# Third layer's attention with scores as split products, two heads side by side in the rows of the array, and the division of the probabilities on GpSimd

## The reference, cut to what matters

```python
q = (rms_norm(c_q, q_norm_w) @ w_uq).reshape(b, l, 16, 64 + 32)
kv = (rms_norm(c_kv, kv_norm_w) @ w_ukv).reshape(b, l, 16, 64 + 64)
q = jnp.concatenate([q_nope, rope(q_pe)], axis=-1)
k = jnp.concatenate([k_nope, jnp.broadcast_to(rope(k_pe), (b, l, 16, 32))], axis=-1)
s = jnp.einsum('bqhd,bkhd->bhqk', q, k) * (96 ** -0.5)
p = jax.nn.softmax(s, axis=-1)
return jnp.einsum('bhqk,bkhd->bqhd', p, v)
```

## Time and profile before

| what | value |
|---|---|
| median of 3 runs | 1498.38 us (1496.53 to 1502.21) |
| profiled execution: its own time | 1499.47 us |
| its span | 1497.6 us |
| TensorE (PE) busy | 95% of the span |
| VectorE, ScalarE, GpSimd busy | 54%, 44%, 55% |
| mean granted TensorE clock | 0.971 |

### The profile page before, as it was taken

One profiled execution on the slowest core, in us unless ns is written; L12 is line 12 of the kernel. 1 busy time (PEld: TensorE's weight loads), 2 busy tenths in 40 slices (PEclk: granted clock), 3 DMA queues, 4 the chain that ended last, 5 costly groups with the idle time before them and its releaser, 6 DMA issues.

```text
span 1497.6 us, 22626 instructions
## 1 busy us (share of the span) xinstructions
PE 1418.1 (95%) x8800; PEld 1212.4 (81%) x8800; DVE 812.0 (54%) x1554; ACT 666.3 (44%) x1100; POOL 825.7 (55%) x665
## 2 busy tenths in 40 slices
PE   5989999999999999887999999999999999999997
PEld 3868788999988887544878888888878865999997
DVE  3687667777576687567675333321126657332211
ACT  3445655544543133674442322232226376544442
POOL 0533507999864443554435454544446630699995
PEclk9999999999999999888999999999999999999999
DMA  9656605777775652100445555543333320365664
GB/s 367 258 184 232 256 5 195 261 253 253 239 262 186 203 175 85 42 29 1 150 146 197 197 186 195 186 140 90 104 104 101 114 96 1 113 195 186 184 185 125
DMA packets 71322, 242.59 MB, mean 162 GB/s; under 512 B 7472, under 2 KB 13104, under 8 KB 70832
## 3 DMA queue, kind: packets, MB, share of 16 engines
q1 hardware_dynamic: 68800, 237.15, 47.0%
q10 hardware_dynamic: 2416, 4.00, 0.9%
HBM read 239.02 MB, written 1.05 MB: 160 GB/s over the span
## 4 chain that ended last, share of the span: by engine, by line
PE 51%; DVE 3%; ACT 1%; issue 1%; POOL 0%; DMA 0%; DVEq 0%; ACTq 0%
PE bank L547 15%; PE bank L549 14%; PE bank L548 14%; PE cond_a L968 1%; PE bank L968 1%; PE bank L684 1%; PE bank L685 1%; PE bank L976 1%; PE cond_a L1028 1%; PE bank L688 1%; PE bank L988 1%; PE cond_b L988 1%; PE cond_b L976 0%; ACT w_hi L1286 0%; DVE scratch L2585 0%
## 5 line engine op out<-in xcount | busy, mean ns | idle before, releaser
L1794 POOL TENSOR_TENSOR w_lo<-raw,w_hi 128x512 fp32r<-128x512 f32 (+1 forms) x612 | 773.1, 1291 | 630.6 <-ACT w_hi L1286 619.7
L1286 ACT ACTIVATE w_hi<-raw 128x1024 fp32r<-128x1024 f32 (+3 forms) x301 | 308.9, 1029 | 592.5 <-PE bank L549 511.9
L547 PE MATMUL bank<-h_hi,w_hi 128*128 128x256 f32 (+2 forms) x1604 | 524.7, 327 | 5.9 <-DVE h_lo L1856 2.6
L549 PE MATMUL bank<-h_hi,w_lo 128*128 128x256 f32 (+2 forms) x1604 | 521.4, 325 | 0.0
L548 PE MATMUL bank<-h_lo,w_hi 128*128 128x256 f32 (+2 forms) x1604 | 521.3, 325 | 0.0
L547 PEld LDWEIGHTS bank<-h_hi,w_hi 128*128 128x128 f32 (+1 forms) x1604 | 301.9, 188 | 38.0 <-DVE h_lo L1856 5.8
L549 PEld LDWEIGHTS bank<-h_hi,w_lo 128*128 128x128 f32 (+1 forms) x1604 | 301.9, 188 | 26.4
L548 PEld LDWEIGHTS bank<-h_lo,w_hi 128*128 128x128 f32 (+1 forms) x1604 | 302.1, 188 | 26.0
L547 PE MATMUL bank<-hidden_hi,w_hi 128*128 128x256 f32 (+1 forms) x528 | 167.0, 316 | 0.2 <-POOL w_lo L1794 0.2
L548 PE MATMUL bank<-hidden_lo,w_hi 128*128 128x256 f32 (+1 forms) x528 | 166.9, 316 | 0.0
L549 PE MATMUL bank<-hidden_hi,w_lo 128*128 128x256 f32 (+1 forms) x528 | 166.9, 316 | 0.0
(11 more groups left out here) (416 smaller groups left out, 1771.7 us busy)
## 6 DMA issues: line engine op xcount, KB each, us to landing
raw<-in_up SPq DMA_DIRECT2D x132, 512.0 KB, 3.6
ada_w<-in_ada SPq DMA_DIRECT2D x128, 512.0 KB, 4.5
raw<-in_down SPq DMA_DIRECT2D x48, 448.0 KB, 3.4
raw<-in_out SPq DMA_DIRECT2D x24, 512.0 KB, 3.7
raw<-in_down SPq DMA_DIRECT2D x24, 512.0 KB, 3.6
raw<-in_in SPq DMA_DIRECT2D x24, 512.0 KB, 3.6
arena<-in_ada SPq DMA_DIRECT2D x16, 512.0 KB, 11.8
raw<-in_uq SPq DMA_DIRECT2D x12, 384.0 KB, 3.0
```

The lines of the kernel that those rows point to most:

```text
L547: pe.matmul(out, w_h, x_h, start=first, stop=False)
L549: return pe.matmul(out, w_l, x_h, start=False, stop=last)
L1286: act.activation(part_slot(w_hi, f, u), raw_slot(f, u), ACT.Copy).then_inc(s["rounded"], 1)
L1794: pool.tensor_tensor(part_slot(w_lo, f, u)[:, a:b], raw_slot(f, u)[:, a:b], part_slot(w_hi, f, u)[:, a:b].bitcast(F32), ALU.subtract).then ...
```

## The change

In TensorE's score product, the two heads of a pair at the same half of the queries are now done together, and each as split products. The 64 plain rows lie in partitions 0 to 63 for one head and 64 to 127 for the other (as `uk` and `uq` deliver them), and the three products hi*hi, hi*lo, lo*hi of each head use that half of the array's rows. The 32 rotary rows are held apart, for the queries in four blocks of 32 partitions and for the key in four copies, and three more products for each head use the block of 32 rows in which the head's rotary rows lie. So a pair of score products is 12 fp32r matmuls of 512 columns, six for each head, alternating between the heads, where there were two f32 matmuls. Scores are issued in pairs, and a pair waits for both exponentials that free its banks.

The operands are prepared otherwise: ScalarE rounds each product of `uk` (`round_keys`) and of the last eight of `uq` (`spread_queries`) with one copy of the full 128 partitions, and VectorE subtracts to get the low part (`low`, the function of line 1856) and then frees the bank. The rotary parts are rounded and subtracted once for all heads (`turn_k_hi`, `turn_k_lo`: 128x512; `turn_q_hi`, `turn_q_lo`: 128x1024). The four copies of `kpe` into `kh` on ScalarE are gone. The operands take the room of `hidden_hi`, `hidden_lo`, `ckv_hi`, `ckv_lo` and `work_r`.

VectorE's `divide` keeps only the reciprocal; GpSimd multiplies the 128x512 probabilities by it (`tensor_tensor` with the column broadcast), a = 0 to 31 in order, after the low parts of the first three units of `out2`.

The diff with its unchanged lines left out; of the list of semaphores, which gains `latent_hi`, `turn_done` and `att_one` and loses `gn_mid` and `kpe_done`, nothing is shown:

```diff
@@ -328,11 +328,21 @@
-        qh, kh, vl = c(LH, LAT), c(LH, TOK), c(TT, 1024)
+        keys_hi, keys_lo = hidden_hi[:, 0:8, :], hidden_hi[:, 8:16, :]
+        queries_hi = hidden_hi[:, 16:20, :].rearrange("p a (b t) -> p (a b) t", b=2)
+        c.at = 24 * TOK
+        vl = c(TT, 1024)
...
+        turn_q_hi, turn_q_lo = (v.rearrange("p a (b t) -> p (a b) t", b=2) for v in (ckv_hi, ckv_lo))
+        turn_k_hi, turn_k_lo = work_r[:, 1, :], work_r[:, 2, :]
...
+        def queries_lo(p):
+            rows = hidden_hi[:, 20 + p // 2, :] if p < 4 else hidden_lo[:, p // 2 - 2, :]
+            return rows[:, p % 2 * LAT:(p % 2 + 1) * LAT]
@@ -956,17 +966,30 @@
-            def attention(m, a0, heads, q, k, v):
+            def attention(m, a0, heads, v):
...
-                    h, t = head_of(a)
...
+                    p, t = a // 4, slice(a // 2 % 2 * P, (a // 2 % 2 + 1) * P)
...
-                        pe.wait_ge(s["att_e"], a0 + a - 3)
-                    pe.matmul(score_bank(a)[:, :], q(h)[:, t * P:(t + 1) * P], k(h),
-                              start=True, stop=True).then_inc(s["att_s"], 1)
+                        pe.wait_ge(s["att_e"], a0 + a - 2)
+                    plain = ((queries_hi[:, p, t], keys_hi), (queries_hi[:, p, t], keys_lo), (queries_lo(p)[:, t], keys_hi))
+                    for n, (q, k) in enumerate(plain):
+                        for e in range(2):
+                            rows = slice(64 * e, 64 * e + 64)
+                            pe.matmul(score_bank(a + e)[:, :], q[rows, :], k[rows, p, :], start=(n == 0), stop=False)
+                    turned = ((turn_q_hi, turn_k_hi), (turn_q_hi, turn_k_lo), (turn_q_lo, turn_k_hi))
+                    for n, (q, k) in enumerate(turned):
+                        for e in range(2):
+                            at = 32 * ((2 * p + e) % 4)
+                            rows = slice(at, at + 32)
+                            last = pe.matmul(score_bank(a + e)[:, :], q[rows, p // 2, t], k[rows, :],
+                                             start=False, stop=(n == 2), tile_position=(at, 0))
+                            if n == 2:
+                                last.then_inc(s["att_s"], 1)
@@ -989,14 +1012,12 @@
-                for a in range(4):
-                    scores(a)
+                scores(0)
+                scores(2)
...
-                    if a % 2:
-                        for n in (a + 3, a + 4):
-                            if n < count:
-                                scores(n)
+                    if a % 2 and a + 3 < count:
+                        scores(a + 3)
@@ -1256,10 +1277,8 @@
-            pe.wait_ge(s["kpe_done"], 4)
-            pe.wait_ge(s["rope_out"], 1)
-            attention(att2, 2 * AH, LH, lambda h: qh[0:LQ, h, :], lambda h: kh[0:LQ, h, :],
-                      lambda h, i: vl[:, i, h * LV:(h + 1) * LV])
+            pe.wait_ge(s["turn_done"], 2)
+            attention(att2, 2 * AH, LH, lambda h, i: vl[:, i, h * LV:(h + 1) * LV])
@@ -1740,34 +1759,37 @@
-                if u == 1:
+                if u == 2:
...
-                if u in (1, 2, 4, 5):
-                    q = (1, 2, 4, 5).index(u)
-                    act.activation(kh[LN:LQ, 4 * q:4 * q + 4, :], kpe[LN:LQ, :].unsqueeze(1).to_broadcast([LR, 4, TOK]),
-                                   ACT.Copy).then_inc(s["kpe_done"], 1)
...
-            def query_scale(u):
-                if u == 1:
-                    act.wait_ge(s["lq_sum"], 1)
-                    act.activation(token_std[:, 0:2], bank[7][:, 0:2], ACT.Sqrt, scale=1.0 / 768, bias=EPS)\
-                       .then_inc(s["lq_std"], 1)
+                    act.activation(turn_k_hi, kpe, ACT.Copy).then_inc(s["latent_hi"], 1)
...
+            def round_keys(u):
...
+                f = ph["uk"]
+                for p in range(4 * u, 4 * u + 4):
+                    act.wait_ge(s["steps"], f.first_step + p + 1)
+                    act.activation(keys_hi[:, p, :], bank_of(f.first_taken + p)[:, :], ACT.Copy).then_inc(s["latent_hi"], 1)
+                round_next()
...
-                if u == 4:
-                    act.wait_ge(s["taken"], f.first_taken + 4)
...
-                b = bank_of(f.first_taken + u)
-                act.activation(qh[0:LN, 2 * u - 8, :], b[0:LN, 0:LAT], ACT.Copy)
-                act.activation(qh[0:LN, 2 * u - 7, :], b[LN:P, 0:LAT], ACT.Copy).then_inc(s["taken"], 1)
+                act.activation(queries_hi[:, u - 4, :], bank_of(f.first_taken + u)[:, 0:LAT], ACT.Copy)\
+                   .then_inc(s["latent_hi"], 1)
+                if u == 6:
+                    act.wait_ge(s["rope_out"], 1)
+                    act.activation(turn_q_hi, rope_q, ACT.Copy).then_inc(s["latent_hi"], 1)
...
-            phase("uk", query_scale)
+            round_keys(0)
+            round_keys(1)
+            act.wait_ge(s["lq_sum"], 1)
+            act.activation(token_std[:, 0:2], bank[7][:, 0:2], ACT.Sqrt, scale=1.0 / 768, bias=EPS)\
+               .then_inc(s["lq_std"], 1)
@@ -1839,6 +1861,13 @@
+            if layers > 2:
+                lows(ph["out2"].first_unit + SLOTS)
+                for a in range(2 * LH):
+                    pool.wait_ge(s["att_one"], a + 1)
+                    prob = att2["prob"][a % 4]
+                    pool.tensor_tensor(prob, prob, att2["total"][:, a:a + 1].to_broadcast([P, TOK]), ALU.mult)\
+                        .then_inc(s["att_p"], 1)
@@ -2289,9 +2318,7 @@
-                    then(dve.reciprocal(one, one))
-                    dve.tensor_scalar(m["prob"][a % 4], m["prob"][a % 4], one, None, ALU.mult)\
-                       .then_inc(s["att_p"], 1)
+                    dve.reciprocal(one, one).then_inc(s["att_one"], 1)
@@ -2652,7 +2679,7 @@
-                        return copy(kpe[LN:LQ, :], b[LN:LQ, :])
+                        return copy(kpe, b[:, :])
@@ -2661,11 +2688,11 @@
-                k_lat, k_swap = kpe[LN:LQ, L0:L1], kswap[LN:LQ, :]
-                then(dve.stream_shuffle(k_swap, k_lat, swap16))
-                dve.tensor_tensor(k_lat, k_lat, cs[LN:LQ, :], ALU.mult)
-                then(dve.tensor_tensor(k_swap, k_swap, sn[LN:LQ, :], ALU.mult))
-                dve.tensor_tensor(k_lat, k_lat, k_swap, ALU.add).then_inc(s["kpe_in"], 1)
+                k_lat = kpe[:, L0:L1]
+                then(dve.stream_shuffle(kswap, k_lat, swap16))
+                dve.tensor_tensor(k_lat, k_lat, cs, ALU.mult)
+                then(dve.tensor_tensor(kswap, kswap, sn, ALU.mult))
+                dve.tensor_tensor(k_lat, k_lat, kswap, ALU.add).then_inc(s["kpe_in"], 1)
@@ -2705,11 +2732,13 @@
+                dve.wait_ge(s["latent_hi"], 1)
+                low(turn_k_lo, kpe, turn_k_hi).then_inc(s["turn_done"], 1)
...
-                    copy(kh[0:LN, 2 * p, :], b[0:LN, :])
-                    return copy(kh[0:LN, 2 * p + 1, :], b[LN:P, :])
+                    dve.wait_ge(s["latent_hi"], 2 + p)
+                    return low(keys_lo[:, p, :], b[:, :], keys_hi[:, p, :])
@@ -2728,11 +2757,23 @@
+                def plain_query(p):
...
+                    product_in(f, 4 + p)
+                    dve.wait_ge(s["latent_hi"], (10 if p < 3 else 11) + p)
+                    low(queries_lo(p), bank_of(f.first_taken + 4 + p)[:, 0:LAT], queries_hi[:, p, :])\
+                       .then_inc(s["taken"], 1)
...
-                for q in range(4):
-                    a, b = 32 * q, 32 * q + 32
-                    last = dve.tensor_tensor(qh[LN:LQ, q::4, :], rope_q[a:b, :, :], swapped[a:b, :, :], ALU.subtract)
-                last.then_inc(s["rope_out"], 1)
+                plain_query(0)
+                dve.tensor_tensor(rope_q, rope_q, swapped, ALU.subtract).then_inc(s["rope_out"], 1)
+                plain_query(1)
+                plain_query(2)
+                dve.wait_ge(s["latent_hi"], 13)
+                low(turn_q_lo, rope_q, turn_q_hi).then_inc(s["turn_done"], 1)
+                for p in range(3, 8):
+                    plain_query(p)
```

More of the change, by code:

```diff
@@ L360, in build @@
             "swap_done", "log_ready", "rt_sum", "sd_sum", "rt_s", "rt_e", "rt_p", "rt_o", "rt_y",
-            "gn_mid", "gn_inv", "gn_in", "gn_sum", "gn_spread", "gn_std", "gn_act", "gn_done", "dt_cols", "dt_ready", "dt_log", "gn_gate", "sd_t", "sd_tt", "sd_b", "sd_s",
+            "gn_inv", "gn_in", "gn_sum", "gn_spread", "gn_std", "gn_act", "gn_done", "dt_cols", "dt_ready", "dt_log", "gn_gate", "sd_t", "sd_tt", "sd_b", "sd_s",
             "sd_arg", "sd_e", "sd_p", "sd_o", "sd_y", "sn_in", "sn_sq", "sn_acc", "sn_sum", "sn_std", "sn_inv", "sn_spread",
             "lk_sq", "lk_in", "lk_sum", "lk_std", "lk_inv", "lk_spread", "lk_work", "lk_hi", "lk_done",
-            "lq_act", "lq_lo", "lq_in", "lq_sum", "lq_std", "lq_scale", "rope_out", "kpe_in", "kpe_done"]
+            "lq_act", "lq_lo", "lq_in", "lq_sum", "lq_std", "lq_scale", "rope_out", "kpe_in", "latent_hi", "turn_done", "att_one"]
         s = {n: sem(n) for n in names}
```

## The result

The changed kernel takes 1511.1 us (median of 7 runs, 1507.5 to 1517.5), the kernel before 1502.2 us (median of 7, 1495.9 to 1506.3): ratio 1.0067, 95% interval 1.0049 to 1.0085. By the ratio that is 10.0 us more, with an interval from 7.4 to 12.8 (the medians lie 8.9 apart). Forecast were +9.3 and a time of 1507.7 within 1500.5 to 1518, from a kernel before at 1498.4, and slower by more than 0.5% with a chance of 0.65. The profiled execution took 1514.9 us with a span of 1513.1.

What follows compares the result with a forecast made beforehand. It took the attention stage as bound by TensorE's work. Terms 0.4 + 2.3 + 1.5 + 0.4 + 3.0 + 2.2 - 0.5 gave +9.3 us: 1508.8 profiled, 1507.7 as median, range 1500.5 to 1518.

Steps and rivals of the forecast that it cites:

- three changes of division: In each score pair: full rows to 64, 64 to 32, 32 to the next product; 0.18 us each, 0.54 in all.
- the prediction's signs: Profile after: pairs 1.9 us, GpSimd 1.27, first turn near 1215, period 7.7, turns waiting for GpSimd, last values 6.7 behind.
- The score pair: TensorE's scores for two heads: six passes side by side, 1.36 us, plus 0.54 for division changes, 1.90 for 1.72.
- One period: Four a in the attention: TensorE's work 7.41 us, about 0.3 waiting for GpSimd, 7.7 for 7.21; six periods lose 3.0.
- Rival 1: Cheap changes and quick GpSimd: pair 1.72, multiplication 1.04, period 7.05, -1.1 over six; +3.6 us, 1502.0; chance 0.16.
- The start: Attention's beginning: first turn at 1214.95 instead of 1213.29, second 1.27 instead of 0.59 later; loss 2.3 us.
- what comes before: Ahead of the start, in `uq`: VectorE's new subtraction and ScalarE's new rounding; loss 0.4 us, bounds 0 and 1.
- The early turns: Third and fourth turn pair, no values' product as cover: 1.5 us lost; two score pairs outside the periods add 0.4.
- The clock: Behind the start's waits: half speed for 3.4 us, a loss of 1.7 us, kept unchanged in the sum.
- rival 3: Longer waits at the end or in each period lower the clock once or twice more, 1.7 us each: 1510 to 1512; chance 0.07.
- The end: Last score pair's end to last values: 6.75 us instead of 4.5, with two GpSimd products; loss 2.2.
- Ahead of the attention: Before `uk`: `kpe`'s four copies leave ScalarE, TensorE's 1.19 us wait shrinks; gain 0.5, bounds 0 and 1.19; `uk` subtractions covered.
- VectorE's 128x1024 subtraction: In `uq`, ahead of the start: 2 x 1.77 = 3.5 us beside a busy GpSimd.

Runs made afterwards that it cites:

- a_warm: Changed kernel plus 18 unused fp32r matmuls in TensorE's two waits at the start (6 and 12): ratio 1.0045 to the kernel before, 69.76 us from first scores to `out2`.
- b_warm: Kernel before plus 11 unused matmuls in TensorE's two waits at the start (4 and 7): ratio 0.9993 to the kernel before, 63.10 us from first scores to `out2`.
- a_64rows: Changed kernel with rotary products over 64 rows instead of 32, computing other scores: 69.75 us from first scores to `out2`; no time ratio.
- a_dve: Changed kernel with the division of the probabilities back on VectorE: ratio 1.0040 to the kernel before; 68.84 and 69.34 us from first scores to `out2`.
- b_pool: Kernel before with only the multiplications of the division moved to GpSimd: ratio 1.0018 to the kernel before, 67.34 us from first scores to `out2`.
- a_dve_warm: Changed kernel with the division back on VectorE and 15 unused matmuls in the start's waits (6 and 9): ratio 1.0021 to the kernel before, 67.48 us.
- a_row: Changed kernel with the 12 products reordered, three of one head before three of the other: 74.53 us from first scores to `out2`; no time ratio.
- a_mid: Changed kernel plus 8 unused full-row matmuls behind the third score pair, none in the start's waits: 74.85 us from first scores to `out2`; no time ratio.

## Why the prediction was right

The time was right, and the mechanism for the most part: divided rows that run side by side, three changes of division, GpSimd's latency at both ends. That the sum came as near as 9.3 to 10.0 is partly luck. At full clock the stage lost 6.7 us (a_warm against b_warm) where the sum has 9.8 for it, and the half clock, which the sum left as it was, put 1.8 on top in the mean of two profiles each. The gain ahead of the attention came as forecast, but a wait in `uk`, costed at nothing, took it back. Of the prediction's signs, the pairs, the first turn and the slower period came; GpSimd's 1.27 us, turns that wait for it in the middle, and 6.7 us at the end did not.

- **The score pair**, 1.90 forecast: 1.78 between the turns plus 0.15 on the turn behind it, 1.93. That heads run side by side held, and so nearly did 0.18 a change, 0.57 for the three: the plain part takes 0.21 more than its three passes, the change from 64 to 32 rows, for which there was no row, costs 0.18 (a_64rows), the way back 0.15. The split saves no time because what six passes save against two f32 matmuls (1.72 - 1.36 = 0.36 us) is less than the 0.57 of the changes.
- **One period**, 7.7 forecast, 7.50 measured. TensorE's own work was forecast at 7.41 and fills all of the 7.50. The term that was mis-sized is GpSimd's multiplication: 1.27 us taken, 1.04 measured. With it the 5.5 us to the odd turn are 5.05, less than TensorE's 5.25 of cover, and the forecast 0.3 us of waiting a period is not there (a_dve and b_pool: period unchanged by where the division is). Five periods cost 1.4 us for 2.5; the sum had six whole ones (3.0), while the trace has only five between the first and the sixth values. (Rival 1's -1.1 over six periods is -1.0 by its own 7.05.)
- **The start**: first turn 2.05 us later against the first scores; forecast 1.65, plus part of the 0.4 for what comes before. The second pair started 3.34 us after the first for 2.93, 0.4 later. From there to the first turn it took 5.26 us, where 5.28 were forecast, but that is two errors that cancel: GpSimd's 0.2 less, and a second pair that took 2.24 us (1212.93 to 1215.17), because the clock fell within it. At full clock the first turn comes 1.67 us later (a_warm against b_warm). The early turns: 2.55 forecast with the second turn and the two extra pairs, 1.8 measured at full clock (the same two runs).
- **The clock**: the sum kept the loss of the kernel before. Measured between first turn and first values, half clock took 14.38 - 10.03 = 4.4 and 12.66 - 10.03 = 2.6 us in the changed kernel and 9.77 - 8.25 = 1.5 and 1.7 in the kernel before. So 1 to 3 us are missing from the sum: rival 3's loss, but at the start and not at the end, where the clock stayed at 1.00. It makes up for part of the waits that GpSimd's shorter time takes out of the sum.
- **The end**: from the end of the last score pair to the last values 6.75 forecast, 6.15 measured (1274.85 to 1281.00), so 1.6 lost for 2.2; GpSimd's 0.23 us less, twice, account for most of it. The 1.75 of the table hold also 0.11 for the last score pair.
- **Ahead of the attention**: a gain of 0.5 forecast, 0.58 and 0.66 measured from the norm to `uk` (42.74 before, 42.16 and 42.08 after). But `uk` was costed at nothing, and there TensorE waits 0.71 us for its first bank, which VectorE takes out behind the 1.53 us of `turn_k_lo`; the first scores start 0.75 us later against the beginning of `uk` in both profiles of the changed kernel. The cover of 1.4 us a product was right for each product, but not for the one behind the new subtraction.

By cause, at full clock (6.7 us from first scores to `out2`): the split scores 4.4 (a_dve_warm), GpSimd's division 2.3. The half clock adds 1.8 us on average. That TensorE's waits start it is shown (a_warm, which fills both and so doesn't tell one from the other). Its length goes with the wait ahead of the first turn: with 1.6 us (before) it is 3.4 and 6.8, with 2.2 (b_pool) 6.8, with 2.5 (a_dve) 6.8 twice, with 3.0 to 3.1 (changed, a_row, a_mid, a_64rows) 10.2 to 17.1. The two halves of the change lengthen this wait together, which would explain why they cost more together than apart; that is argued from one or two profiles of each kernel. Why the half clock then lasts that long while TensorE is busy is open. a_mid speaks against the want of full-row work; a_64rows, with 10.2 us, stands between, in one profile.

## What to carry to other kernels

A product split in three passes beats a plain f32 one only by what its passes save (here 0.36 us a pair) less the changes of row division around it (here 0.57); count these changes per group of products, not per kernel, and group what uses the same division. Work handed to an idle slower engine was free in the middle of this pipeline, where TensorE had other work to cover it, and cost 2.3 us at its two ends, where nothing did. And a wait on TensorE can cost twice: around waits of 1.5 and 3 us the granted clock was at half for 13.7 to 17.1 us. Look at the granted clock behind a wait, and fill it with unused matmuls if nothing better is to be had (74.3 and 73.0 us became 69.8).

## What the runs showed of the hardware that was not expected

- Two heads' products in different rows of the array run side by side also when three of one head are issued before three of the other: 1.80 against 1.78 us a pair. The Trainium skill ("TensorE: Matmul & The Clock Gate", The mechanism) says that matmuls stay in strict order of issue. The trace of this run does not agree: its records have the first two products of the second head ahead of the third of the first (1250.02 x4, then 1250.58 x2), and if each product had to wait for the start of the one before it, only the last of one head and the first of the other could run side by side: five passes, 5 x 0.227 = 1.13 us, for a plain part that took 0.90. In what order the products went into the array, the records alone tell.
- GpSimd's 128x512 product of a tensor with a broadcast column takes 1.04 us, as that of a tensor with itself, and not 1.27 as with two full tensors.
- Behind waits of TensorE at the same place the granted clock was at half for 3.4 and 6.8 us in one kernel and for 13.7 and 17.1 us in the other, TensorE being busy for most of it.
- VectorE's 128x1024 subtraction beside a busy GpSimd, forecast at 3.5 us from the 1.77 for 128x512, took 1.91 (`turn_q_lo`).
